# One encoder layer in float32, one core: x1 is added into the rows of the down projection by seven accumulating DMAs from GpSimd

## The reference

```python
h = rmsnorm(x1, ffn_norm_g[i])
x = x1 + swiglu(h, ffn_w_gate_up[i], ffn_w_down[i])   # w_down: 5632 x 2048
```

## Time and profile before

| | |
|---|---|
| median of 3 runs | 2135.71 us (2135.28 to 2136.56) |
| the profiled execution, its own time | 2136.44 us |
| its span, first to last instruction | 2134.7 us |
| busy, ScalarE | 944.6 us (44%) |
| busy, GpSimd | 174.2 us (8%) |
| mean granted TensorE clock | 0.998 |
| DMA | 376.31 MB, mean 176 GB/s |

### The profile page before, as it was taken

One profiled execution on the slowest core, in us unless ns is written; L12 is line 12 of the kernel. 1 busy time (PEld: TensorE's weight loads), 2 busy tenths in 40 slices (PEclk: granted clock), 3 DMA queues, 4 the chain that ended last, 5 costly groups with the idle time before them and its releaser, 6 DMA issues. The chain is left out here.

```text
span 2134.7 us, 27909 instructions
## 1 busy us (share of the span) xinstructions
PE 2113.3 (99%) x10404; PEld 1845.4 (86%) x10404; DVE 1526.2 (71%) x2108; ACT 944.6 (44%) x1281; POOL 174.2 (8%) x354
## 2 busy tenths in 40 slices
PE   8999999999999999999999999999999999999998
PEld 8999999999998888888888888888888777887876
DVE  4444444444455435888888987987978998999999
ACT  5333333333343335444444444544445554544533
POOL 0322222222221000000000000000000000000000
PEclk9999999999999999999999999999999999999999
DMA  6232333232243344666666666676677877868766
GB/s 185 76 99 79 93 85 92 79 98 79 84 128 128 119 134 132 198 218 200 219 212 211 208 219 212 204 233 204 198 235 232 269 256 246 263 208 269 260 186 203
DMA packets 258924, 376.31 MB, mean 176 GB/s; under 512 B 15842, under 2 KB 114180, under 8 KB 258324
## 3 DMA queue, kind: packets, MB, share of 16 engines
q1 hardware_dynamic: 255456, 354.90, 52.8%
q10 hardware_dynamic: 3380, 20.21, 2.5%
HBM read 346.45 MB, written 28.61 MB: 176 GB/s over the span
## 5 line engine op out<-in xcount | busy, mean ns | idle before, releaser
L1391 DVE TENSOR_TENSOR f_lo<-f_raw,f_hi 128x1536 fp32r<-128x1536 f32 (+1 forms) x230 | 454.4, 1980 | 46.9 <-ACT f_hi L1020 31.4
L564 PE MATMUL gemm<-w_hi,act_t 128*128 128x384 f32 (+2 forms) x1280 | 450.7, 352 | 2.3 <-DVE w_lo L1207 2.3
L565 PE MATMUL gemm<-w_lo,act_t 128*128 128x384 f32 (+2 forms) x1280 | 443.9, 347 | 0.0
L566 PE MATMUL gemm<-w_hi,act_t 128*128 128x384 f32 (+2 forms) x1280 | 443.9, 347 | 0.0
L765 PE MATMUL gemm<-f_hi,a_form 128*128 128x512 f32 x1056 | 411.2, 389 | 0.0
L767 PE MATMUL gemm<-f_hi,a_form 128*128 128x512 f32 x1056 | 411.1, 389 | 0.0
L766 PE MATMUL gemm<-f_lo,a_form 128*128 128x512 f32 x1056 | 410.8, 389 | 0.0
L765 PE MATMUL aux<-f_hi,a_form 128*128 128x512 f32 x792 | 313.2, 395 | 6.7 <-DVE f_lo L1391 5.1
L1207 DVE TENSOR_TENSOR w_lo<-w_raw,w_hi 128x768 fp32r<-128x768 f32 (+1 forms) x160 | 160.7, 1008 | 208.5 <-ACT w_hi L862 208.5
L766 PE MATMUL aux<-f_lo,a_form 128*128 128x512 f32 x792 | 308.5, 390 | 0.0
L767 PE MATMUL aux<-f_hi,a_form 128*128 128x512 f32 x792 | 308.5, 390 | 0.0
(11 more groups left out here) (184 smaller groups left out, 2227.5 us busy)
## 6 DMA issues: line engine op xcount, KB each, us to landing
f_raw<-in_ffn_w_gate_up SPq DMA_DIRECT2D x264, 512.0 KB, 4.2
f_raw<-in_ffn_w_down SPq DMA_DIRECT2D x132, 512.0 KB, 4.8
w_raw<-in_fox_w_in SPq DMA_DIRECT2D x192, 256.0 KB, 3.3
f_raw<-in_ffn_w_gate_up SPq DMA_DIRECT2D x88, 256.0 KB, 4.0
w_raw<-in_fox_w_out SPq DMA_DIRECT2D x16, 1024.0 KB, 5.1
f_raw<-in_ffn_w_down SPq DMA_DIRECT2D x44, 256.0 KB, 4.9
a_raw<-forms_scratch SPq DMA_DIRECT2D x22, 512.0 KB, 6.6
forms_scratch<-fa_a ACTq DMA_DIRECT2D x11, 896.0 KB, 6.3
```

What stands on the lines that cost most here:

```text
L564: mm(out, a_hi, b_hi, start=first, stop=False)
L565: mm(out, a_hi, b_lo, start=False, stop=False)
L566: return mm(out, a_lo, b_hi, start=False, stop=last)
L1391: v.tensor_tensor(f_lo[:, n % 4, 0:3 + g], f_raw[:, n % 4, 0:3 + g], f32(f_hi[:, n % 3, 0:3 + g]), ALU.subtract).then_inc(f_lo_done, 1)
```

## The change

Pieces 0 to 6 are no longer loaded into a buffer by SyncE and added by VectorE. GpSimd issues seven DMAs whose source is `dram_x1` and whose destination is the part of `rows` itself, with accumulation. Three go out when round 11's sums are in `rows` (column groups 0 and 2), three after round 12's (groups 1 and 3), and the last, group 2's second half, after `last_bottom` in round 16. `add_p2` waits for the three of its group pair; the store of that last piece waits for its own semaphore. Piece 7 stays as it was. The buffer x1_piece, its waits and ScalarE's wait for three pieces go.

```diff
-        PIECES = [((0, 0), (R_DOWN + 1, 0, 2), (R_DOWN + 1, 0, 1)),
-                  ((0, 1), (R_DOWN + 1, 0, 3), (R_DOWN + 1, 0, 2)),
-                  ((2, 0), (R_DOWN + 1, 0, 4), (R_DOWN + 1, 0, 3)),
-                  ((1, 0), (R_DOWN + 2, 1, 5), (R_DOWN + 2, 1, 5)),
-                  ((1, 1), (R_DOWN + 3, 0, 2), (R_DOWN + 3, 0, 3)),
-                  ((3, 0), (R_DOWN + 3, 0, 4), (R_DOWN + 3, 0, 6)),
-                  ((2, 1), (R_DOWN + 5, 0, 4), (R_DOWN + 5, 0, 2)),
-                  ((3, 1), (R_DOWN + 5, 1, 5), (R_DOWN + 5, 1, 6))]
...
+        X1_PIECES = [((0, 0), (0, 1), (2, 0)), ((1, 0), (1, 1), (3, 0))]
...
-                if n in PIECE_LOAD:
-                    k = PIECE_LOAD[n]
-                    d, half = PIECES[k][0]
-                    src = dram_x1[d][:, 2 * half:2 * half + 2]
-                    if k == 0:
-                        for m in range(ND):
-                            sp.wait_ge(x1_stored[m], 16)
-                        for i in range(2):
-                            sp.wait_ge(forms_stored[i], 16 * NP)
-                    if k < 3:
-                        sp.dma_start(early_piece(k), src).then_inc(early_ld[k], 16)
-                    elif k < 7:
-                        sp.wait_ge(piece_added, k)
-                        sp.dma_start(x1_piece[:], src).then_inc(piece_ld, 16)
-                    else:
-                        sp.wait_ge(x1_p2, 4)
-                        sp.dma_start(p2_kept[:], src).then_inc(last_piece_ld, 16)
+                if n == BASE[R_DOWN + 5] + ROUND_K[R_DOWN + 5] + 6:
+                    sp.wait_ge(x1_p2, 4)
+                    sp.dma_start(p2_kept[:], dram_x1[3][:, 2:4]).then_inc(last_piece_ld, 16)
...
-            sp.wait_ge(piece_added, 7)
+            sp.wait_ge(x1_added_late, 16)
             sp.dma_start(y_cols[2][:, 2:4], rows[:, 2, 2:4]).then_inc(y_stored, 16)
...
+            for d in range(ND):
+                pool.wait_ge(x1_stored[d], 16)
+            for n in range(2):
+
+                r = R_DOWN + n
+                pool.wait_ge(x1_p1, n + 1)
+                pool.wait_ge(x4_p1, n + 1)
+                pool.wait_ge(x2_p5, 2 * n + 2)
+                pool.wait_ge(p7_read, 2 * r + 2)
+                for d, half in X1_PIECES[n]:
+                    pool.dma_start(rows[:, d, 2 * half:2 * half + 2], dram_x1[d][:, 2 * half:2 * half + 2],
+                                   accum_op=ALU.add).then_inc(x1_added[n], 16)
+            pool.wait_ge(c_out, 2)
+            pool.wait_ge(x2_x4, 2)
+            pool.dma_start(rows[:, 2, 2:4], dram_x1[2][:, 2:4], accum_op=ALU.add).then_inc(x1_added_late, 16)
...
-                    act.wait_ge(piece_added, 3)
...
                 dve.wait_ge(p2_read, 2 * r + 2)
+                dve.wait_ge(x1_added[n], 48)
                 x1 = rows[:, n, 0:2]
...
-            def add_piece(k):
-                d, half = PIECES[k][0]
-                if k < 3:
-                    dve.wait_ge(x1_p1, 1)
-                    dve.wait_ge(early_ld[k], 16)
-                    piece = early_piece(k)
-                else:
-                    dve.wait_ge(piece_ld, 16 * (k - 2))
-                    piece = x1_piece[:]
-                part = rows[:, d, 2 * half:2 * half + 2]
-                v.tensor_tensor(part, part, piece, ALU.add).then_inc(piece_added, 1)
...
-                if (r, g, j) in PIECE_ADD and PIECE_ADD[r, g, j] < 7:
-                    add_piece(PIECE_ADD[r, g, j])
```

More of the change, by code:

```diff
@@ L109, in encoder_layer @@
         p3_kept = at("p3_kept", AREA_A + 7 * 14336 + 4096, [P, 2, CW])
-        x1_piece = at("x1_piece", AREA_A + 7 * 14336 + 8192, [P, 2, CW])
         a_raw = [at(f"a_raw{j}", AREA_A + 14336 * j + 7168, [P, 7, HW]) for j in range(8)]
@@ L230, in encoder_layer @@
         x1_stored = [sem(f"x1_stored{d}") for d in range(ND)]
-        piece_ld, piece_added = sem("piece_loaded"), sem("piece_added")
-        early_ld = [sem(f"early_piece_loaded{k}") for k in range(3)]
+        x1_added = [sem("x1_added0"), sem("x1_added1")]
+        x1_added_late = sem("x1_added_late")
+        piece_added = sem("piece_added")
         last_piece_ld = sem("last_piece_loaded")
@@ L1563, in last_products @@
                     dve.wait_ge(p5_p6, t + 1)
-                    dve.wait_ge(piece_added, 8)
+                    dve.wait_ge(piece_added, 1)
                     x4 = rows[:, 3, 2 + t]
```

## The result

The changed kernel takes 2151.2 us (median of 4 runs, 2149.16 to 2152.09), the kernel before 2135.49 us (4 runs): a ratio of 1.0065, 95% interval 1.0053 to 1.0077. It is slower by 15.7 us, well outside the range. The profiled execution took 2152.09 us, its span is 2150.3 us, 15.6 us more than before.

The account below looks back on a forecast made before the run. TensorE, busy 2113.3 us of a 2134.7 us span, was taken as the bound. 2136.44 - 0.54 + 0.8 + 0.4 = 2137.1 us for the profiled execution, 2136.4 us for a median; range 2133.9 to 2142.0 us.

Parts of the forecast that it names:

- What bounds the kernel, and VectorE's relief: Down stage: TensorE can win back only its 4.5 us of waits and a little tail; VectorE loses 8.5 us of adds.
- The gain of 0.54 us at 1950 us: Round 14: without piece 5 VectorE is earlier, so TensorE's 0.54 us wait at 1950 us goes; bounds 0 to 0.54 us.
- three transfers at once: About 1785 and 1862 us: bursts exceed free DMA time by 1.2 and 1.4 us, costing 0.8 and 0.4 us.
- The price: Three accumulating pieces at a load's cost take 4.9 us of engine time; at double, 9.8 us; the lower was taken.
- 3.8 us of slack: At g = 0 units: loads go out 12.1 us ahead, land in 4.8 us, hi and lo take about 3.5 us.
- The late transfer: About 2077.5 us: 0.52 MB takes 1.6 us and fits 2.5 us free, cost 0; at the upper end 0.8 us.
- Rival C: First g = 1 units: accumulating transfers starve weight loads, 3 to 4 us late each, about +6 us, 2142 us; chance 0.20.
- sign of being wrong: Accumulating transfers landing in 15 us or more would show the prediction wrong; within 10 us of issue was expected.
- B: Down stage: bursts are hidden by 3.8 us of slack and only gains stay, 2134.2 us; chance 0.20.
- D: Down stage: all of TensorE's waits go as VectorE keeps 8.5 us of slack, 2130.2 us; chance 0.03.
- E: Down stage: GpSimd's issue holds VectorE up, 1.6 us above the sum, 2138 us; chance 0.09.
- The new waits: add_p2 of rounds 13 and 14, at least 25 us after issue, and the late piece's store: nothing waits.

Follow-up runs that it names:

- e3_loads_no_adds: The kernel before with its seven x1 loads kept but VectorE's seven adds left out (output incomplete); ratio 0.999 (0.998 to 1.000).
- e4_spaced: The changed kernel with its six grouped accumulating transfers issued one at a time, 2 units apart in first passes; ratio 1.0029 (1.0019 to 1.0040) to the kernel before.
- e5_small_packets: The changed kernel with each of six grouped transfers cut in two by token tile, packets of 2048 bytes; ratio 1.0068 (1.0052 to 1.0083) to the kernel before.
- e9_low_single: The changed kernel with its six grouped transfers issued singly in second passes of rounds 13 and 15, where DMA share is low; ratio 1.0013 to the kernel before.
- e2_plain_pool: The changed kernel with its seven GpSimd transfers overwriting rows without accumulation (sums lost); ratio 1.0013 (1.0004 to 1.0023) to the kernel before.
- e8_early_small: The changed kernel with transfers issued singly, early in the passes, each cut in two by token tile; ratio 1.0027 (1.0016 to 1.0038) to the kernel before.
- e10_low_burst: The changed kernel with each group's three transfers at once in second passes of rounds 13 and 15, where DMA share is low; ratio 1.0045 to the kernel before.
- e7_early: The changed kernel with transfers issued singly, placed before loads of the first g = 1 units go out; ratio 1.0025 (1.0014 to 1.0036) to the kernel before.

## Why the prediction was wrong

- **What bounds the kernel, and VectorE's relief.** Right in size: TensorE could win little, and it did not. VectorE's total fell by 7.3 us, where 8.5 us was forecast. The gain of 0.54 us at 1950 us was credited to the wrong cause: e3_loads_no_adds keeps the wait, and in the one execution without the load as well it is gone.
- **The step that failed** is the sum for "three transfers at once": what does not fit into the free engine time (1.2 and 1.4 us), less the slack, gave 0.8 and 0.4 us. The runs showed a wait of 5.25 us and one of 5.38 us. Two terms were mis-sized. The price: I took the lower end, 4.9 us of engine time for three pieces; measured were 7.9 us, and 64.6 / 16 = 4.0 us without accumulation. The exchange: I let the transfers have only the idle part of the engines, as if the loads went first. They do not. Inside the first burst the loads got 78 GB/s where they need some 190, so that they fell further behind for as long as it lasted, some 10 us.
- **The place was wrong too.** The sum let the burst bite at the first g = 1 units, with slacks of 0.1 and 0.4 us, and left out the g = 0 units, to which the prediction gave 3.8 us of slack. Both waits stand at g = 0 units, and the g = 1 units behind them, at 1816.76 and 1898.42 us, start without one. The slack did not hold: in the DMA view of 1785 to 1805 us the 256 KB loads, which only g = 0 units have, land after 11.6 us, where in the same window of the kernel before it was 4.9 us (first line: the changed kernel, second: the kernel before).

```profile
f_raw<-in_ffn_w_down SPq DMA_DIRECT2D x3, 256.0 KB, 11.6
...
f_raw<-in_ffn_w_down SPq DMA_DIRECT2D x3, 256.0 KB, 4.9
```

- **The late transfer** landed within 5.9 us, and no wait of TensorE follows it. Its 0 in the sum was right.
- **A term was missing:** the lower clock that came with a stop of 5 us, 2.7 us the first time. Before, the down stage ran at 1.00 throughout apart from its tail, so no row of it had this price. It makes the loss more than proportional: in e4_spaced, with waits of at most 1.35 us, it is absent until the tail.
- **Rival C** named the mechanism, accumulating transfers that starve the weight loads, and had 0.20. It had the place wrong like the sum, the first g = 1 units, and it held against itself that the g = 0 loads have slack, the very loads that failed. Its 3 to 4 us a group, without the clock, gave 2142 us; the real 2151.2 us lies beyond. It let the loads have half of each engine; they got 23.1% inside the first burst. The landings speak against the sum: none of the six grouped transfers landed within 10 us of its issue, and the last of each group, with 15.3 and 16.3 us, passed the 15 us that the prediction had named as a sign of being wrong.
- The Trainium skill ("DMA: Bandwidth & Descriptors", Queues, rings and completion order) lets each DMA engine go round between queues by packets, which C cites. The traces agree as far as they can tell: inside the burst the two queues moved 397 and 358 packets, and halving the accumulating packet in e5_small_packets raised the loads' rate from 78 to 117 GB/s and shortened the longest waits. But turns by packets are not equal halves of the time when one queue's packet takes 330 ns.
- **The rivals B, D, E** fell. E, GpSimd's issues holding VectorE up: a lo half beside the issues takes 1.76 us, the same as elsewhere.

```profile
1787.12 1.76 DVE L1377 TENSOR_TENSOR f_lo<-f_raw,f_hi 128x1536 fp32r<-128x1536 f32 x1 [0.72 <-ACT f_hi L1007]
```

- **The new waits** (add_p2, the store) cost nothing, as said.

Open: how much of the remaining 1.0013 of e9_low_single is the transfers' engine time and how much their place; the runs' spread hides it.

## What to carry to other kernels

An accumulating DMA is not a free add: here it held the DMA engines twice as long as a plain transfer of the same bytes, and its packets shared the engines with loads that had a deadline. Before moving work from an engine to DMA, compare the slack of the loads it will meet with the whole length of the burst, not with the idle share, and don't send several at once: here that cost more at both places tried. Where TensorE is the bound, a stop of some microseconds can cost its length and then the slow matmuls after it.

## What the runs showed of the hardware that I had not expected

- Packets of 4096 bytes into `rows` took about 330 ns with accumulation, 168 ns without; packets of 2048 bytes with it, 180 ns.
- DMA engines at a full share moved 252 to 276 GB/s during the accumulation and 403 GB/s just after.
- TensorE's granted clock was at 0.50 for about 7 us, beginning about a microsecond or two before the end of the stops of 5.25 and 5.38 us. Shorter stops gave no clear order. With stops of 2.10 us (e9_low_single), 2.42 us (e2_plain_pool), 2.67 us (e8_early_small), 2.80 and 3.10 us (e5_small_packets), 2.99 and 3.62 us (e10_low_burst) it was at 0.50 for about 3 us. With stops of 2.37 us (e5_small_packets) and 2.62 us (e7_early) it stayed at 1.00.
